# Setting the prompt's compression products between the mixer's last projection units

## What is computed

```python
def compress(rows, w1, w2, pe):
    ...
    chunks = rows[:, :n_chunks * CMP_STRIDE].reshape(b_, n_chunks, CMP_STRIDE, KV_HEADS, HEAD_DIM)
    part = jnp.einsum('bcsgd,rsdh->bcrgh', chunks, w1)
    hid = jnp.einsum('rsd,rsdh->h', pe.reshape(CMP_RATIO, CMP_STRIDE, HEAD_DIM), w1)
    for r in range(CMP_RATIO):
        hid = hid + part[:, r:r + n_cmp, r]
    return jax.nn.silu(hid) @ w2
```

## Time and profile before

| | |
|---|---|
| median of three runs | 1428.47 us (1427.21 to 1428.62) |
| profiled execution, its own time | 1427.87 us |
| its span | 1426.1 us |
| PE busy | 1383.0 us, 97% of the span |
| DVE, ACT, POOL busy | 623.5, 518.2, 546.3 us |
| mean granted TensorE clock | 0.988 of full speed |

### The profile page before, as it was taken

The page is one execution under the profiler, slowest core; times in us unless marked ns, Lnnn a source line. Parts: engine busy times, 40 slices in busy tenths (PEclk is TensorE's granted clock), DMA queues, the critical chain, the costliest instruction groups (busy, mean ns, idle before and its releaser), DMA issues.

```text
span 1426.1 us, 27186 instructions
## 1 busy us (share of the span) xinstructions
PE 1383.0 (97%) x11546; PEld 1329.2 (93%) x11546; DVE 623.5 (44%) x948; ACT 518.2 (36%) x797; POOL 546.3 (38%) x274
## 2 busy tenths in 40 slices
PE   7999999999999999998989999998999999999998
PEld 7999899999999999997855579998999999999997
DVE  4677333430133475297477731224843240023352
ACT  5676622221122322113367743323343431122221
POOL 4330344443344443432034334444444453244440
PEclk9999999999999999999999999999999999999999
DMA  8531122341222342333343433322222242232311
GB/s 296 206 119 59 60 89 88 103 133 59 86 92 96 125 163 89 89 114 98 105 177 127 171 93 101 101 91 89 89 89 89 88 133 75 82 95 88 110 38 60
DMA packets 116419, 151.72 MB, mean 106 GB/s; under 512 B 4646, under 2 KB 111370, under 8 KB 114244
## 3 DMA queue, kind: packets, MB, share of 16 engines
q1 hardware_dynamic: 113820, 117.17, 25.9%
q0 software_dynamic: 2304, 33.56, 6.3%
q10 hardware_dynamic: 232, 0.09, 0.0%
HBM read 147.05 MB, written 7.95 MB: 109 GB/s over the span
## 4 chain that ended last, share of the span: by engine, by line
PE 90%; DVE 6%; ACT 2%; DMA 1%; issue 1%; SPq 0%; ACTq 0%; DVEq 0%
PE bank L1663 72%; PE bank L1604 7%; PE bank L1538 6%; PE bank L1775 1%; ACT sm L893 1%; DVE tmp L1164 1%; PE bank L1556 1%; PE bank L1802 1%; PE bank L1831 1%; DMA GB<-cache_sel_kv,idx 1%; DVE ui L1184 1%; PE bank L1858 1%; DMA w<-w_cmpk 0%; DVE tmp L1062 0%; PE bank L1846 0%
## 5 line engine op out<-in xcount | busy, mean ns | idle before, releaser
L590 POOL TENSOR_TENSOR wlo<-raw,whi 128x1024 fp32r<-128x1024 f32 (+3 forms) x182 | 458.1, 2519 | 662.1 <-ACT whi L712 661.7
L712 ACT ACTIVATE whi<-raw 128x1024 fp32r<-128x1024 f32 (+3 forms) x183 | 196.4, 1076 | 676.0 <-PE bank L1663 656.7
L1663 PE MATMUL bank<-xh,whi 128*128 128x260 f32 (+1 forms) x2032 | 411.5, 284 | 1.2 <-DVE tmp L1164 0.7
L1663 PE MATMUL bank<-xh,wlo 128*128 128x260 f32 (+1 forms) x2032 | 410.6, 284 | 0.0
L1663 PE MATMUL bank<-xl,whi 128*128 128x260 f32 (+1 forms) x2032 | 410.1, 283 | 0.0
L1663 PEld LDWEIGHTS bank<-xh,whi 128*128 128x128 f32 (+1 forms) x2032 | 313.8, 189 | 2.8 <-issue 1.3
L1663 PEld LDWEIGHTS bank<-xh,wlo 128*128 128x128 f32 (+1 forms) x2032 | 313.8, 189 | 0.3
L1663 PEld LDWEIGHTS bank<-xl,whi 128*128 128x128 f32 (+1 forms) x2032 | 312.9, 188 | 0.3
L1121 DVE TENSOR_TENSOR tmp<-bank,rr 128x520 f32<-128x520 f32 x88 | 61.6, 700 | 284.0 <-PE bank L1663 283.6
L1663 PE MATMUL bank<-hl,whi 128*128 128x260 f32 x704 | 141.9, 283 | 0.0
L1663 PE MATMUL bank<-hh,wlo 128*128 128x260 f32 x704 | 141.6, 282 | 0.0
(11 more groups left out here) (324 smaller groups left out, 1743.3 us busy)
## 6 DMA issues: line engine op xcount, KB each, us to landing
raw<-ffn_w_gate SPq DMA_DIRECT2D x22, 1024.0 KB, 5.4
raw<-ffn_w_up SPq DMA_DIRECT2D x22, 1024.0 KB, 5.3
raw<-w_mix_in SPq DMA_DIRECT2D x17, 1024.0 KB, 5.1
raw<-ffn_w_down SPq DMA_DIRECT2D x8, 1536.0 KB, 6.5
raw<-ffn_w_down SPq DMA_DIRECT2D x8, 1280.0 KB, 5.7
GB<-state_win_kv SPq DMA_DIRECT2D x8, 512.0 KB, 5.6
raw<-w_mix_out SPq DMA_DIRECT2D x4, 1024.0 KB, 5.4
win_kv_sample<-state_win_kv SPq DMA_DIRECT2D x1, 4088.0 KB
```

The lines of the kernel that those rows point to most:

```text
L590: pool.tensor_tensor(tile(wlo, w, k, u), raw_tile(u), tile(whi, w, k, u).bitcast(F32), ALU.subtract)\
L712: act.activation(dst, src, ACT.Copy).then_inc(hi_done, 1)
L1663: ins = pe.matmul(acc(g)[0:m, h, :], w[:, u % WS, c, 0:m], x[:, c, h * HT:(h + 1) * HT], start=(c == 0 and n == 0), stop=(c == k - 1 and n ...
```

## The change

The two compression products leave their place behind the gates' turns and the four tiny products. The keys' product is now issued right behind unit 20 and the values' right behind unit 21, each with the same 16 products as before, on the same operands and the same bank. The taking of the ring's first place is replaced by a direct use of its bank, and the wait for the weights and for `xtp` goes with the products. The counter that tells ACT that both are done is counted up at the end of the second, now ahead of unit 22. Nothing is added, removed or moved on any other engine.

```diff
+            def prompt_hidden(kk):
+
+                out = bank[:, rbank("hid"), :]
+                pe.wait_ge(xtp_ready, 1)
+                pe.wait_ge(w1p_loaded[kk], (64, 16)[kk])
+                for r in range(2):
+                    for s in range(8):
+                        j = 8 * r + s
+                        w = w1pv[:, j, :] if kk else w1pk[j // 4][:, j % 4, :]
+                        ins = pe.matmul(out[:, 64 * kk:64 * kk + KVH * PCMP].rearrange("p (g c) -> p g c", g=KVH), w,
+                                        xtp[kk][:, s, :, r:r + PCMP], start=(r + s == 0), stop=(r == 1 and s == 7))
+                return ins
+
             for t in range(16, 23):
                 unit(U_M1 + t, xh, xl)
...
+                if t in (20, 21):
+                    ins = prompt_hidden(t - 20)
+                    if t == 21:
+                        ins.then_inc(ring_full, 1)
...
-            out = claim("hid")
-            pe.wait_ge(xtp_ready, 1)
-            for kk in range(2):
-                pe.wait_ge(w1p_loaded[kk], (64, 16)[kk])
-                for r in range(2):
-                    for s in range(8):
-                        j = 8 * r + s
-                        w = w1pv[:, j, :] if kk else w1pk[j // 4][:, j % 4, :]
-                        ins = pe.matmul(out[:, 64 * kk:64 * kk + KVH * PCMP].rearrange("p (g c) -> p g c", g=KVH), w,
-                                        xtp[kk][:, s, :, r:r + PCMP], start=(r + s == 0), stop=(r == 1 and s == 7))
-            ins.then_inc(ring_full, 1)
             pe.wait_ge(tp_ev, 7)
             sample_keys(0)
```

More of the change, by code:

```diff
@@ L1705, in _, with claim @@
                     unit(U_M1 + j, xh, xl, i, 4)
+            def claim(*label):
+                n = RING.index(label)
+                if n >= 3:
+                    pe.wait_ge(*emptied(*RING[n - 3]))
+                return bank[:, 5 + n % 3, :]
+            def prompt_hidden(kk):
[9 more added lines that the diff above has]
+                return ins
             for t in range(16, 23):
@@ L1756, in _ @@
             ins.then_inc(new_done, 1)
[L1758 to L1763, removed]
             def scores(p, tiles=(3, 2, 0, 1)):
```

## The result

| | before | after |
|---|---|---|
| median of five runs | 1427.21 us | 1435.33 us |
| lowest, highest | 1425.84, 1428.62 | 1433.9, 1438.84 |
| profiled execution, its span | 1426.1 us | 1432.1 us |
| PE busy in it | 1383.0 us | 1383.7 us |

The ratio is 1.0058, with a 95% interval of 1.0046 to 1.0070. The change costs about 8 us, and PE does the same work as before, in 0.7 us more of busy time. The forecast was 1435.6. The profiled execution of the changed kernel is the fastest of its five (1433.9 us), 6.0 us above the profiled one of the kernel before (1427.87), so its trace shows less of the loss than the median has.

A forecast was written before the change was run, and what follows sets the result against it. PE, busy 97% of the span, was taken to bound the kernel. A 7.6 us shift less 2.1 of earlier slack makes 5.5; with 2.2 for the clock, 7.7 on 1427.87 gives 1435.6 us, range 1432.4 to 1438.8.

The forecast's parts named there:

- What bounds the kernel, and the hidden wait: PE bounds; before the window's turns, the compression products covered a row copy arriving 5.0 us after they began.
- The products in their new place: Behind units 20 and 21: no wait for inputs or weights, no gaps to fill, the full 7.29 us.
- The seams: Breaks in the units' stream at the products' new place: 0.3 us in all, bounds 0 and 0.7.
- The wait: Before the window's turns PE waits 5.0 us for the fourth row copy; the turns begin 5.5 us later.
- The shift: Everything behind unit 22, up to the tiny products, and the row copies run 7.6 us later.
- The clock: Behind PE's idle time the window's turns run at half clock: 2.2 us lost, bounds 0 and 10.7.
- What is queued behind: Turns, scores, first gather and prompt attention behind PE's idle time: all shift, nothing gives the loss back.
- the long low stretch: Rival: PE waits and half clock lasts through the second window's turns, 5.1 us; 1438.5 us, chance 0.16.
- The short stretch: Likeliest case: PE waits before the window's turns, then one low-clock period costs 2.2 us; 1435.6 us, chance 0.60.
- The held clock: Rival: PE waits 5.0 us before the window's turns but keeps full clock; 5.5 us lost, 1433.4 us, chance 0.16.
- The not-slower case: Rival: row copies are not late, reached within 2.4 us of the tiny products; loss at most 2.9 us, chance 0.08.

The follow-up runs named there:

- the cut products: The kernel before with 1 of the 16 products of each compression left at the old place; 1429.55 us, ratio 0.9996.
- the busy wait: The changed kernel with 27 products that nobody reads put into PE's wait ahead of the window's turns; 1432.83 us, ratio 1.0028.
- one copy: The changed kernel with one copy of four rows per window in place of four copies of one row; 1431.68 us, ratio 1.0035.
- the scores: The changed kernel with the first prompt scores (12 products) put ahead of the window's turns instead of behind the second window's; 1431.35 us, ratio 1.0018.

## Why the prediction was right

*What bounds the kernel, and the hidden wait:* right. The argument that the products covered an arrival 5.0 us behind their beginning was borne out by the wait in the changed kernel, by its shrinking with the copies, and by the cut products.

*The products in their new place:* right that nothing waits for them. The seams were mis-sized: 0.3 us taken, but the mask's product behind unit 22 begins 7.09 us later than before (24.64 against 17.55 from the reference point), and the products themselves take 7.04 on the chain. The seams cost nothing that can be told. The products take 3.52 us each on the chain where 3.6 to 3.8 were forecast, and the values' begins at 688.21 where 688.3 was.

*The wait:* mechanism right, size 4.0 us instead of the 5.0 forecast, and the turns 4.0 us later instead of 5.5. The shift made 0.5 of it: the tiny products end at 30.33 us from the reference point, where the turns began before. The rest is the fourth copy: it took 2.8 us to land in the kernel before, 1.70 in the changed one. I had carried one landing over as if it were fixed. The eight landings of the kernel before, in order, are 2.4, 1.9, 2.2, 2.8, 2.4, 1.7, 1.7 and 1.7 us, which was there to be read; what stands beside the 2.8 is told in the last section.

The Trainium skill, DMA: Bandwidth & Descriptors, Anatomy of one DMA — SWDGE (gpsimd) path, has about 2.0 us as fixed cost, which would have given a wait of 4.2. It is stated there for transfers that GpSimd issues, while these come from SP's queue, and the traces have 1.7 to 2.9 us for them.

*The clock:* mechanism right; the 2.2 us were 1.3 at the turns in the profiled execution, and 3 to 4 in the median, by the busy wait. The mean granted clock says the same: 0.9861 over 35 executions of the kernel before and 0.9836 over the 12 of the changed kernel timed beside them. 0.0025 of 1432 us are 3.6 us of full-clock time (an estimate, and a high one, since waits inside a low stretch count in it); with the wait of 4.0 that makes 7.6 of the 8.0 us between the medians. That the sum of 7.7 came so near the measured 8.1 is thus partly luck: 1.5 us too much for the wait and its shift, and about as much too little for the clock. The forecast of 1435.6 also starts from 1427.87, which is 0.7 above the median of 1427.21 that the five executions gave.

*What is queued behind:* the loss is passed on in full, as forecast: in the profiled execution the second window's turns, the scores and the compressed scores all stand 5.3 us later, and the first gather is issued at 719.80 instead of 714.60, where about 722 was forecast. That ACT's SiLU gains nothing was right for the changed kernel. Without the row copies it becomes a wait of its own, 0.74 us.

*The rivals:* the long low stretch is what the second profiled execution of the changed kernel shows, and its price was right: 5.1 us at the softmax's turns, as forecast. Its chance was not: it had 0.16, and six of the twelve executions have the time and the clock that go with it. The short stretch, which had 0.60 and 2.2 us, costs 1.3. The short and the long stretch are thus not rival accounts but executions of one kernel, and the median lies between them. The held clock was seen in the traces only with a shorter wait (one copy) or with work in it (the busy wait, the scores), not in either trace of the changed kernel. The not-slower case fell with the 4.0 us.

## What to carry to other kernels

Work that stands between a producer and a consumer on another engine may be the cover of a wait that no view shows. Before moving it, list what the next instruction behind it waits for and when each of those arrives, and compare with the end of the instruction in front of it, not with the end of the cover. A chain of small copies issued one by one belongs in that list with its last landing. And count what a wait does to the clock of the work behind it, which may be as much as the wait itself.

## What the runs showed of the hardware that was not expected

The same wait of 4.0 us was followed by 3.41 us at the low clock in one execution and by 13.66 us in another of the same kernel. So a profiled execution gives one draw of that cost, and single executions of one kernel spread over 7 us (1432.49 to 1439.56).

The clock also fell after waits that I would have called short: 1.73 us with only the keys' product moved, and 0.55 and 0.74 us without the row copies. In the kernel before it fell even after a stretch which the profile counts as busy throughout, with narrow products of 8 to 64 columns up to 844.02 and the first products of a unit behind them (stretches of that kernel):

```profile
841.61:845.02 3.41, 3.41 (x30) 3.34 (x30) 0.51 (x3) 0.79 (x3) 0.00 (x0) 1.00 0.23 81
845.02:848.43 3.41, 3.41 (x18) 3.41 (x17) 0.83 (x2) 3.38 (x4) 2.61 (x2) 0.50 0.00 0
```

Whether in the short-wait cases it was the wait or the thin work around it that let the clock fall was not separated.

A small copy's way from issue to landing depended on what was in SP's queue ahead of it. In both traces of the changed kernel the first row copy, right behind the two stores of 256 KB, lands after 2.4 us, the second after 1.9 and the other six after 1.7. One copy of four rows took 2.30 us behind the stores and 1.83 ahead of them.

The longer landings in the kernel before go with a transfer of instructions of 0.02 MB on queue q8. It begins at 698.60 us, between the issues of the fourth copy (698.20) and the fifth:

```profile
698.83 1.30 SPq L506 DMA_DIRECT2D GB<-srows  x1
```

The fourth copy lands after 2.8 us, and the fifth takes 1.30 us to issue instead of 0.59. With the small products first on the kernel before it is the same (2.9 us, and 1.47 us to issue). With the keys' product only, the transfer meets the second store, which takes 1.93 us to issue. In the changed kernel it begins at 699.44, about 4 us before the first copy, and with the products cut there is none near the copies: there the fourth lands after 1.7 us. So the landing that the forecast carried over was lengthened by something that did not move with the products. No run moved such a transfer by itself, so that it is the cause is likely but not shown.
